# A three-stage block on one core: merge gates biased during the choosing of keys, two of them loaded early, joining's first two tiles reordered

## The chip, the core and the metric

The kernel runs on one core of a Trainium2 chip. The core has TensorE (matrix products, called PE in the profile, with its weight loads apart as PEld), VectorE (DVE), ScalarE (ACT), GpSimd (POOL), and SyncE (SP), which here only issues transfers. All five run their own instruction lists and meet at semaphores. The metric is device time in microseconds for one execution of the whole program, as a median over runs. Before the change it is 3973.13 us over 3 runs (3967.18 to 3975.65).

## The reference

Two transformer blocks in a row, in float32, over 1024 rows of 1024 columns. Only the first block's middle is touched:

```python
proj = jnp.matmul(h, w_in[l])
(fq, fk, fv, flog, dq, dk, dv, iq, ik, iw, g_fox, g_dsa) = jnp.split(proj, split_at, axis=-1)
...
merged = (jax.nn.sigmoid(g_fox + b_gate[l, :D]) * jnp.matmul(out_fox, w_proj_fox[l])
          + jax.nn.sigmoid(g_dsa + b_gate[l, D:]) * jnp.matmul(out_dsa, w_proj_dsa[l]))
x = x + gt1 * jnp.matmul(merged, w_out[l])
h2 = rmsnorm(x, norm2_g[l]) * (1.0 + sc2) + sh2
```

The gates `g_fox` and `g_dsa` are 2048 columns of `proj`. A routed mixture of 32 experts and a second block follow.

## The kernel before

The rows are cut into NT = 8 tiles of 128, the columns into chunks of CH = 512. Each stage is a block with one hand-written program for each engine, and all engines meet at a barrier between two stages. The order of work is the order in which these programs are written; there is no planner except the table of `side_work`.

**choose** (214 to 678 us of the profile) finds the 256 best keys of each row. DVE does it: for each tile, 32 rounds of MAX8 (L667) and MATCH_REPLACE8 (L668), and `gather` (L649, L652) adds up the next tile's scores between them. PE has little to do for this, so `side_work` gives it 64 tasks on the side: 8 small ones, and 7 chunks of `proj` by 8 tiles. The last four chunks (tasks 32 to 63) are the gates. Each task is 8 products of 128x512 (16 in the profile's count), a copy by ACT into one of four buffers `ch_out`, and a store to DRAM issued by ACT (L601). POOL meanwhile weighs the 8 chunks of a vector-matrix product in four steps each (L628 to L634), and PE turns each result into columns (`turn`). The stage is over when ACT has seen all stores land and DVE has read the last turned columns.

**attending** (678 to 996 us) runs two attentions, 32 units each (the sparse one, then the forgetting one, `fox`), through DVE, ACT and PE. SP loads `w_proj` when the sparse half's scores are reduced, one `plain` tile (the forgetting decay) for each tile of the second half, and `w_out` in two pieces of 2 MB, the second after the last unit (L772).

**joining** (997 to 1338 us) works tile by tile. `merge(t, c)` is 8 products (L1190) for column half c, which the profile counts as 16, `mix(t, c)` on DVE (L1390 to L1393) multiplies them by the opened gates and adds the two; `flip_m(t)` transposes the result on PE (L1200), `project(t, c)` multiplies it by `w_out` (L1213), `residual` on DVE adds it to x, ACT squares it and takes the root, `scale_rows` on DVE scales it, `flip_x` transposes it (L1223), and `logit` scores it for the router. The gate of a tile goes through SP (load), POOL (`bias_gate`, L1336) and ACT (`open_gate`, the sigmoid, L1291). In DVE's gaps `weigh` (L1417, L1420) builds the second block's modulation from chunks `w_mod` of 2 MB, loaded by SP one after the other into a single buffer, each when the one before has been weighed (`load_mod`, L1160): one chunk for each tile, and a second one for odd tiles.

**experts** (1338 us on) reads its first weights into `space` and `aT`, which SP loads in joining's last part.

## Time and profile before

| what | value |
|---|---|
| median of 3 runs | 3973.13 us (3967.18 to 3975.65) |
| the profiled execution | 3977.49 us, of which its span is 3975.5 us |
| PE busy | 3741.8 us, 94% of the span |
| DVE, ACT, POOL busy | 1737.1, 952.4, 458.2 us |
| granted clock of PE, mean | 0.947 of full speed |

"Busy" is the sum of an engine's instruction times. Two parts matter here: the end of choose (660 to 680 us) and the start of joining (995 to 1075 us). Each is read on a timeline, engine by engine: start, duration, what it is, and in brackets how long the engine stood idle before it and what released it. The granted clock is 1.00 at full speed (2.4 GHz) and 0.50 at the lower level (1.2 GHz).

### The profile page before, as it was taken

To read this page: it belongs to the slowest core of one execution; us is meant where nothing else is said; L and a number is where in the kernel's file an instruction comes from. 1 tells how busy PE (TensorE), PEld (TensorE's weight loads), DVE (VectorE), ACT (ScalarE), POOL (GpSimd) and SP (SyncE) were. 2 spreads that over 40 slices of the span, in tenths; PEclk is the share of its full clock that TensorE was granted. 3 is DMA by queue.
4 is the path that set the end of the run, shared out by engine and by line. 5 is a ranking of instruction groups with operands and counts; after the bars stand their busy time and mean duration, and the time that the engine had idled before them with its cause. 6 is when DMAs were issued, how large, how long until landed. Compare 5 with 4: busy or idle time off the path is not lost. (4 is left out here: it accounts for less than half of the span.)

```text
span 3975.5 us, 45903 instructions
## 1 busy us (share of the span) xinstructions
PE 3741.8 (94%) x18108; PEld 1997.1 (50%) x18108; DVE 1737.1 (44%) x2905; ACT 952.4 (24%) x1981; POOL 458.2 (12%) x348
## 2 busy tenths in 40 slices
PE   6999999999799699999977999999898999999999
PEld 3554444555455444444435457876655444444444
DVE  2479998655455100000012334555353343343246
ACT  2311111544122122222113312222243311111001
POOL 0032231311210211010111111211000000000000
PEclk8979999999899799999986999999899999999999
DMA  4213232121645489898956222222113111111434
GB/s 172 74 35 119 77 138 81 30 61 36 219 146 194 166 335 335 330 341 328 342 201 236 90 71 88 94 81 86 52 35 116 41 43 43 43 43 43 130 109 158
DMA packets 294008, 533.04 MB, mean 134 GB/s; under 512 B 24132, under 2 KB 103060, under 8 KB 291518
## 3 DMA queue, kind: packets, MB, share of 16 engines
q1 hardware_dynamic: 272574, 472.17, 34.3%
q0 software_dynamic: 11952, 43.52, 2.7%
...
q14 instruction: 54, 0.44, 0.0%
...
## 5 line engine op out<-in xcount | busy, mean ns | idle before, releaser
L561 PE MATMUL ch_side<-aT,space 128*128 128x512 f32 x896 | 391.9, 596 | 0.0
L1738 DVE TENSOR_SCALAR ex_y<-ex_y,ex_entry 128x1024 f32<-128x1024 f32 x32 | 41.1, 1284 | 639.7 <-PE ex_y L1658 639.7
L561 PEld LDWEIGHTS ch_side<-aT,space 128*128 128x128 f32 x896 | 168.9, 191 | 213.2 <-issue 210.5
L1642 PE MATMUL ex_a<-space,ex_xT 128*128 128x512 f32 x512 | 228.5, 600 | 6.2 <-ACT ex_xT L1709 6.2
L2962 PE MATMUL en_bank<-en_h,en_up 128*128 128x512 f32 x528 | 233.8, 593 | 0.0
L1658 PE MATMUL ex_y<-aT,ex_actT 128*128 128x512 f32 x512 | 227.9, 599 | 0.7 <-ACT ex_actT L1721 0.7
L1642 PE MATMUL ex_b<-space,ex_xT 128*128 128x512 f32 x512 | 225.0, 593 | 0.0
L2124 PE MATMUL mx_duo<-mx_chunks,mx_region 128*128 128x512 f32 x384 | 183.6, 635 | 0.0
L667 DVE MAX8 ch_best<-ch_score 128x8 f32<-128x384 f32 (+5 forms) x192 | 171.6, 894 | 6.1
L668 DVE MATCH_REPLACE8 ch_score<-ch_best,ch_score 128x384 f32<-128x384 f32 (+5 forms) x192 | 168.1, 875 | 0.0
L1642 PEld LDWEIGHTS ex_a<-space,ex_xT 128*128 128x128 f32 x512 | 98.5, 193 | 130.3 <-issue 130.3
L2962 PEld LDWEIGHTS en_bank<-en_h,en_up 128*128 128x128 f32 x528 | 100.4, 190 | 125.6 <-issue 125.6
L2962 PE MATMUL en_bank<-en_h,en_mixed_up 128*128 128x512 f32 x352 | 158.3, 593 | 0.0
L2071 PE MATMUL mx_duo<-mx_late 64*64 64x64 f32 (+1 forms) x3632 | 146.7, 226 | 6.8 <-DVE mx_late L2703 5.7
L1658 PEld LDWEIGHTS ex_y<-aT,ex_actT 128*128 128x128 f32 x512 | 96.0, 193 | 109.8 <-issue 108.7
L1642 PEld LDWEIGHTS ex_b<-space,ex_xT 128*128 128x128 f32 x512 | 95.0, 190 | 107.5 <-issue 107.5
L1709 ACT ACTIVATE ex_xT<-ex_x,modT,ex_gain 128x128 f32<-128x128 f32 x264 | 95.6, 467 | 206.3 <-PE ex_x L1647 206.3
L2071 PEld LDWEIGHTS mx_duo<-mx_late 64*64 64x64 f32 (+1 forms) x3632 | 121.9, 136 | 35.4 <-issue 30.7
L3257 DVE TENSOR_TENSOR en_region<-en_region,en_bank 128x512 f32<-128x512 f32 x88 | 58.5, 685 | 157.9 <-PE en_bank L2962 66.6
L2126 PE MATMUL mx_duo<-mx_chunks,mx_region 128*128 128x256 f32 x512 | 123.2, 396 | 4.4 <-DMA mx_chunks<-w_in 4.4
L3257 DVE TENSOR_TENSOR en_part<-en_part,en_bank 128x512 f32<-128x512 f32 x88 | 58.5, 686 | 151.5 <-ACT en_part L3133 75.5
L2128 PE MATMUL mx_duo<-mx_region,mx_chunks 128*128 128x512 f32 x256 | 119.8, 623 | 4.5 <-DMA mx_chunks<-w_in 4.5
...
## 6 DMA issues: line engine op xcount, KB each, us to landing
space<-exp_w SPq DMA_DIRECT2D x64, 2048.0 KB, 12.6
aT<-exp_w SPq DMA_DIRECT2D x32, 2048.0 KB, 13.9
en_up<-w_down SPq DMA_DIRECT2D x132, 256.0 KB, 3.6
space<-w_ada SPq DMA_DIRECT2D x12, 2048.0 KB, 8.3
mx_x<-proj_padded SPq DMA_DIRECT2D x96, 256.0 KB, 3.6
space<-ada_w SPq DMA_DIRECT2D x8, 2048.0 KB, 14.1
aT<-w_in SPq DMA_DIRECT2D x7, 2048.0 KB, 8.6
proj<-ch_out ACTq DMA_DIRECT2D x56, 256.0 KB, 2.0
```

What stands on the lines that cost most here:

```text
L561: last = nc.tensor.matmul(side_ps[i % 2][:, 0:width], hT[:, k, t * P:(t + 1) * P], by[:, k, 0:width], start=k == 0, stop=k == KD - 1)
L667: chain(nc.vector.max(best[:, :], sc))
L668: chain(nc.vector.match_replace(sc, best[:, :], sc, CHOSEN))
L1642: last = nc.tensor.matmul(ps[:, :], xT[b][:, k, :], w13[b][s][:, k, :], start=k == 0, stop=k == KD - 1)
L1658: last = nc.tensor.matmul(y_ps[:, c:c + CH], actT[:, k, :], w2[b][:, k, c:c + CH], start=k == 0, stop=k == F // P - 1)
L1709: last = nc.scalar.activation(xT[b][:, k, :], x_ps[:, k, :], ACT.Identity, bias=shift[:, k:k + 1], scale=gain[:, k:k + 1])
L2071: mm = lambda out, a, b, start=True, stop=True: nc.tensor.matmul(out, a, b, start=start, stop=stop)
L2124: last = nc.tensor.matmul(ps[:, :], hT[:, k, t * P:(t + 1) * P], w_qkv[c][:, k, :], start=k == 0, stop=k == KD - 1)
L2126: last = nc.tensor.matmul(ps[:, 0:256], hT[:, k, t * P:(t + 1) * P], w_half[c][:, k, :], start=k == 0, stop=k == KD - 1)
L2128: last = nc.tensor.matmul(ps[:, :], w_half[c // 2][:, k, (c % 2) * P:(c % 2 + 1) * P], hT[:, k, t * CH:(t + 1) * CH], start=k == 0, stop=k ...
L2962: last = nc.tensor.matmul(to[:, :], a[:, k, :], b[:, k, :], start=k == 0, stop=k == HK - 1)
L3257: TT(C[a][b], C[a][b], up_bank(i, m)[:, :], op).then_inc(joined, 1)
```

## The change

1. In choose, POOL adds the bias to each gate task's output in `ch_out` before it is stored (`add_bias`, 32 times 128x512). SP, not ACT, issues these 32 stores. POOL's weighing steps are now tied to the tasks: step s of vector n follows task 8 + 7n + 1 + s. The bias, 1 MB, is loaded at choose's start and no longer at joining's.
2. In attending, the gates of tile 0 are loaded behind `w_proj`, the gates of tile 1 after the last scores. `w_out` comes in four pieces of 1 MB; the last three are no longer held until the last unit is weighted, only until the last scores.
3. In joining, POOL adds no bias. SP's first load is the first chunk `w_mod`. PE does `merge(1, 0)` before `flip_m(0)`, and DVE weighs its first chunk after `mix(0, 1)`, not before it. The load of the first expert's w1 waits for the second last `project` as well, since the buffers have moved.

```diff
+        gate_bias = sb("gate_bias", [P, 2 * D])
+        bias_loaded, biased = g.sem("ch_bias_loaded"), g.sem("ch_biased")
...
+        gate_at = lambda kind, n: columns[n] - C_GATE if kind == "column" and columns[n] >= C_GATE else None
+        gates = [i for i, (kind, n, t) in enumerate(tasks) if gate_at(kind, n) is not None]
...
+            sp.dma_start(gate_bias[:, :], row_bcast(g.d["b_gate"][0], 2 * D)).then_inc(bias_loaded, 16)
             for i, (kind, n, t) in enumerate(tasks):
+                if i in gates:
+                    c = columns[n]
+                    sp.wait_ge(biased, gates.index(i) + 1)
...
-                act.wait_ge(side_copied, i + 1)
-                act.dma_start(rows(g.d["proj1"])[:, t, c:c + width], out[i % OUTS][:, 0:width]).then_inc(stored[i % OUTS], 16)
+                if i not in gates:
+                    act.wait_ge(side_copied, i + 1)
+                    act.dma_start(rows(g.d["proj1"])[:, t, c:c + width], out[i % OUTS][:, 0:width]).then_inc(stored[i % OUTS], 16)
...
-            for n in range(len(vectors)):
-                pool.wait_ge(g.vector_loaded, 16 * (n + 1))
-                if n >= 2:
-                    pool.wait_ge(turned, n - 1)
-                TT = nc.gpsimd.tensor_tensor
-                TT(w_vector, w_vector, g.cT[:, 0:KD].unsqueeze(2).broadcast_to([P, KD, CH]), ALU.mult).then_inc(weighed, 1)
-                pool.wait_ge(weighed, 4 * n + 1)
-                TT(w_vector[:, 0:4, :], w_vector[:, 0:4, :], w_vector[:, 4:8, :], ALU.add).then_inc(weighed, 1)
-                pool.wait_ge(weighed, 4 * n + 2)
-                TT(w_vector[:, 0:2, :], w_vector[:, 0:2, :], w_vector[:, 2:4, :], ALU.add).then_inc(weighed, 1)
-                pool.wait_ge(weighed, 4 * n + 3)
-                TT(row[n % 2][:, :], w_vector[:, 0, :], w_vector[:, 1, :], ALU.add).then_inc(weighed, 1)
+
+            def weigh(n, step):
+                if step == 0:
+                    pool.wait_ge(g.vector_loaded, 16 * (n + 1))
+                    TT(w_vector, w_vector, g.cT[:, 0:KD].unsqueeze(2).broadcast_to([P, KD, CH]), ALU.mult).then_inc(weighed, 1)
+                    return
+                pool.wait_ge(weighed, 4 * n + step)
+                if step < 3:
+                    half = KD >> step
+                    TT(w_vector[:, 0:half, :], w_vector[:, 0:half, :], w_vector[:, half:2 * half, :], ALU.add).then_inc(weighed, 1)
+                else:
+                    if n >= 2:
+                        pool.wait_ge(turned, n - 1)
+                    TT(row[n % 2][:, :], w_vector[:, 0, :], w_vector[:, 1, :], ALU.add).then_inc(weighed, 1)
+
+            def add_bias(i):
+                _, n, _ = tasks[i]
+                c = columns[n] - C_GATE
+                if i == gates[0]:
+                    pool.wait_ge(bias_loaded, 16)
+                pool.wait_ge(side_copied, i + 1)
+                TT(out[i % OUTS][:, :], out[i % OUTS][:, :], gate_bias[:, c:c + CH], ALU.add).then_inc(biased, 1)
+
+            for i in range(NT, len(tasks)):
+                if i in gates:
+                    add_bias(i)
+                n, step = divmod(i - NT, 7)
+                if 1 <= step <= 4 and n < len(vectors):
+                    weigh(n, step - 1)
 
         @block.vector
...
+            gate = joining_gates(space)
+            gate_v = rows(g.d["proj1"])[:, :, C_GATE:C_GATE + 2 * D]
...
+            sp.dma_start(gate[0], gate_v[:, 0, :]).then_inc(g.first_gates[0], 16)
...
-            sp.dma_start(w_out[0], out_v[:, :, 0:CH]).then_inc(g.out_loaded[0], 16)
-            sp.wait_ge(weighted, U)
-            sp.dma_start(w_out[1], out_v[:, :, CH:D]).then_inc(g.out_loaded[1], 16)
+            sp.dma_start(w_out[0][0], out_v[:, 0:4, 0:CH]).then_inc(g.out_loaded[0], 16)
+            for a in range(2):
+                sp.wait_ge(scored[a], U)
+            sp.dma_start(gate[1], gate_v[:, 1, :]).then_inc(g.first_gates[1], 16)
+            sp.dma_start(w_out[0][1], out_v[:, 4:8, 0:CH]).then_inc(g.out_loaded[0], 16)
+            for half in range(2):
+                sp.dma_start(w_out[1][half], out_v[:, 4 * half:4 * half + 4, CH:D]).then_inc(g.out_loaded[1], 16)
...
-    w_out = [space[:, a * D:(a + 4) * D].rearrange("p (k n) -> p k n", n=CH) for a in (12, 0)]
+    w_out = [[space[:, a * D:(a + 2) * D].rearrange("p (k n) -> p k n", n=CH) for a in halves] for halves in ((12, 4), (0, 2))]
     return w_proj, w_out
+
+
+def joining_gates(space):
+
+    return [space[:, a * D:(a + 2) * D] for a in (14, 6)]
...
-            load_gate(0)
-            load_gate(1)
...
+            load_mod(0)
...
+            sp.wait_ge(projected, 2 * NT - 1)
...
-                pe.wait_ge(out_loaded[c], 16)
+                pe.wait_ge(out_loaded[c], 32)
...
-            for t in range(NT):
-                merge(t, 0)
+            merge(0, 0)
+            merge(0, 1)
+            merge(1, 0)
+            flip_m(0)
+            for t in range(1, NT):
                 if t >= 2:
+                    merge(t, 0)
                     flip_x(t - 2)
                 merge(t, 1)
                 if t >= 2:
                     logit(t - 2)
-                if t >= 1:
-                    project(t - 1, 0)
+                project(t - 1, 0)
                 flip_m(t)
-                if t >= 1:
-                    project(t - 1, 1)
+                project(t - 1, 1)
...
-                act.wait_ge(biased, t + 1)
+                act.wait_ge(g.first_gates[t % 2], 16)
+                if t >= 2:
+                    act.wait_ge(gate_loaded[t % 2], 16 * (t // 2))
...
-            def bias_gate(t):
-                pool.wait_ge(gate_loaded[t % 2], 16 * (t // 2 + 1))
-                nc.gpsimd.tensor_tensor(gate[t % 2][:, :, :], gate[t % 2][:, :, :], gate_bias[:, :, :], ALU.add).then_inc(biased, 1)
-
-            chain = g.chain(pool)
-            pool.wait_ge(bias_loaded, 16)
-            bias_gate(0)
...
-                if t + 1 < NT:
-                    bias_gate(t + 1)
...
-                weigh("first", t)
+                if t >= 1:
+                    weigh("first", t)
                 mix(t, 1)
+                if t == 0:
+                    weigh("first", t)
...
+            dve.wait_ge(iota, 6)
```

PE at joining's start, before. `jn_bank` are PSUM banks: 0 and 1 take `merge(t, 0)`, 2 and 3 `merge(t, 1)`; the transposes are `flip_m(0)`.

```order
L1190 MATMUL jn_bank1<-dsa,aT 128x512 x4
L1190 MATMUL jn_bank2<-dsa,aT 128x512 [waits proj_loaded1]
L1190 MATMUL jn_bank2<-dsa,aT 128x512 x3
L1190 MATMUL jn_bank3<-dsa,aT 128x512 x4
L1200 MATMUL jn_bank6<-ident,jn_merged0 128x128 [waits jn_mixed]
L1200 MATMUL jn_bank6<-ident,jn_merged0 128x128 x3
L1200 MATMUL jn_bank7<-ident,jn_merged0 128x128 x4
L1190 MATMUL jn_bank0<-dsa,aT 128x512 [waits jn_taken,proj_loaded0]
L1190 MATMUL jn_bank0<-dsa,aT 128x512 x3
```

The same place now.

```order
L1227 MATMUL jn_bank1<-dsa,aT 128x512 x4
L1227 MATMUL jn_bank2<-dsa,aT 128x512 [waits proj_loaded1]
L1227 MATMUL jn_bank2<-dsa,aT 128x512 x3
L1227 MATMUL jn_bank3<-dsa,aT 128x512 x4
L1227 MATMUL jn_bank0<-dsa,aT 128x512 [waits jn_taken,proj_loaded0]
L1227 MATMUL jn_bank0<-dsa,aT 128x512 x3
L1227 MATMUL jn_bank1<-dsa,aT 128x512 x4
L1237 MATMUL jn_bank6<-ident,jn_merged0 128x128 [waits jn_mixed]
L1237 MATMUL jn_bank6<-ident,jn_merged0 128x128 x3
```

The first half of tile 1's merge stands ahead of the transposes of tile 0, and waits for `jn_taken` there.

DVE at the same place, before. The rows with `jn_bank` and `jn_merged` are `mix`, those with `jn_acc` are `weigh`.

```order
L1390 TENSOR_TENSOR space<-space,jn_bank0 128x512 [waits jn_opened,jn_product,chain8528]
L1391 TENSOR_TENSOR space<-space,jn_bank1 128x512
L1393 TENSOR_TENSOR jn_merged0<-space 128x512 [waits jn_taken]
L1417 TENSOR_SCALAR jn_acc0<-space,cT 128x512 [waits jn_mod_loaded]
L1420 SCALAR_TENSOR_TENSOR jn_acc0<-space,cT,jn_acc0 128x512 [waits jn_weighed] x7
L1390 TENSOR_TENSOR space<-space,jn_bank2 128x512 [waits jn_opened,jn_product]
L1391 TENSOR_TENSOR space<-space,jn_bank3 128x512
L1393 TENSOR_TENSOR jn_merged0<-space 128x512 [waits jn_taken]
L1390 TENSOR_TENSOR space<-space,jn_bank0 128x512 [waits jn_opened,jn_product]
```

DVE now.

```order
L1422 TENSOR_TENSOR space<-space,jn_bank0 128x512 [waits jn_opened,jn_product,chain8585]
L1423 TENSOR_TENSOR space<-space,jn_bank1 128x512
L1425 TENSOR_TENSOR jn_merged0<-space 128x512 [waits jn_taken]
L1422 TENSOR_TENSOR space<-space,jn_bank2 128x512 [waits jn_opened,jn_product]
L1423 TENSOR_TENSOR space<-space,jn_bank3 128x512
L1425 TENSOR_TENSOR jn_merged0<-space 128x512 [waits jn_taken]
L1449 TENSOR_SCALAR jn_acc0<-space,cT 128x512 [waits jn_mod_loaded]
L1452 SCALAR_TENSOR_TENSOR jn_acc0<-space,cT,jn_acc0 128x512 [waits jn_weighed] x7
L1422 TENSOR_TENSOR space<-space,jn_bank0 128x512 [waits jn_opened,jn_product]
```

The two `weigh` rows have moved behind the second half of `mix` for tile 0; nothing else of DVE's order changes in this stage but one wait near its end.

POOL in choose, between the weighing of the third and the fourth vector, before. `ch_row` are the weighed rows.

```order
L628 TENSOR_TENSOR space<-space,cT 128x4096 [waits ch_turned,vector_loaded]
L630 TENSOR_TENSOR space<-space 128x2048 [waits ch_weighed]
L632 TENSOR_TENSOR space<-space 128x1024 [waits ch_weighed]
L634 TENSOR_TENSOR ch_row1<-space 128x512 [waits ch_weighed]
L628 TENSOR_TENSOR space<-space,cT 128x4096 [waits ch_turned,vector_loaded]
```

POOL now, from the fourth vector's first step on.

```order
L638 TENSOR_TENSOR space<-space,cT 128x4096 [waits vector_loaded]
L643 TENSOR_TENSOR space<-space 128x2048 [waits ch_weighed]
L655 TENSOR_TENSOR ch_out0<-ch_out0,ch_gate_bias 128x512 [waits ch_side_copied,ch_bias_loaded]
L643 TENSOR_TENSOR space<-space 128x1024 [waits ch_weighed]
L655 TENSOR_TENSOR ch_out1<-ch_out1,ch_gate_bias 128x512 [waits ch_side_copied]
L647 TENSOR_TENSOR ch_row1<-space 128x512 [waits ch_turned,ch_weighed]
L655 TENSOR_TENSOR ch_out2<-ch_out2,ch_gate_bias 128x512 [waits ch_side_copied]
L655 TENSOR_TENSOR ch_out3<-ch_out3,ch_gate_bias 128x512 [waits ch_side_copied]
L655 TENSOR_TENSOR ch_out0<-ch_out0,ch_gate_bias 128x512 [waits ch_side_copied]
L655 TENSOR_TENSOR ch_out1<-ch_out1,ch_gate_bias 128x512 [waits ch_side_copied]
L638 TENSOR_TENSOR space<-space,cT 128x4096 [waits vector_loaded]
```

Between the steps stand the additions of the bias, each behind the copy of its task, so that a step now waits for the tasks ahead of it.

SP across the end of attending and the start of joining, before.

```order
L752 DMA space<-decay_line 128x8x128 [waits ad_restored] x6
L770 DMA space<-w_out 128x8x512 [waits ad_restored]
L772 DMA space<-w_out 128x8x512 [waits ad_weighted]
L76 UNCONDITIONAL_BRANCH
L1141 UNCONDITIONAL_BRANCH [waits barrier_Pool_Activation_PE_DVE_SP_release]
L1149 DMA jn_gate_bias<-b_gate 128x2048
L1144 DMA space<-proj1 128x2048 x2
L1147 DMA jn_x0<-x 128x1024
```

SP now.

```order
L801 DMA space<-w_out 128x4x512 [waits ad_restored]
L804 DMA space<-proj1 128x2048 [waits ad_scored1,ad_scored0]
L805 DMA space<-w_out 128x4x512
L807 DMA space<-w_out 128x4x512 x2
L76 UNCONDITIONAL_BRANCH
L1181 UNCONDITIONAL_BRANCH [waits barrier_Pool_Activation_PE_DVE_SP_release]
L1192 DMA space<-w_ada_2 128x8x512
L1187 DMA jn_x0<-x 128x1024
L1187 DMA jn_x1<-x 128x1024
```

Gates and `w_out` are asked for before the barrier, and the first chunk `w_ada_2` stands first behind it, ahead of x and the router's small tensors.

## Rows read from the trace of the kernel before

**Rows 1.** Windows: stretch, length, then busy us (x instructions) of each engine, PE clock.

```profile
1020.00:1035.00 15.00, 1.54 (x7) 1.54 (x8) 8.56 (x12) 1.91 (x1) 0.37 (x1) 0.50 0.44 153
...
1100.00:1125.00 25.00, 25.00 (x79) 12.85 (x78) 14.28 (x20) 8.81 (x14) 5.63 (x3) 0.93 0.37 124
```

**Rows 2.** Timeline of PE, joining's start: start us, us, what, [idle before <-releaser].

```profile
999.26 13.90 PE L1190 MATMUL jn_bank<-dsa,aT 128*128 128x512 f32 x32
...
1033.46 1.97 PE L1200 MATMUL jn_bank<-ident,jn_merged 128*128 128x128 f32 x8 [20.31 <-DVE jn_merged L1393]
...
1064.77 7.03 PE L1190 MATMUL jn_bank<-dsa,aT 128*128 128x512 f32 x16
...
1072.01 1.09 PE L1223 MATMUL jn_bank<-ident,jn_xn 128*128 128x128 f32 x8 [0.21 <-DVE jn_xn L1408]
```

**Rows 3.** Timeline of ACT, the same stretch.

```profile
997.36 1.28 ACT L1291 ACT_TABLE_LOAD   x1 [2.65 <-PEq L1073]
...
1015.03 1.91 ACT L1291 ACTIVATE space<-space 128x2048 f32<-128x2048 f32 x1 [16.39 <-POOL space L1336]
```

**Rows 4.** Timeline of POOL, the same stretch.

```profile
1010.50 4.50 POOL L1336 TENSOR_TENSOR space<-space,jn_gate_bias 128x2048 f32<-128x2048 f32 x1 [51.40 <-DMA space<-proj]
```

**Rows 5.** Timeline of DVE, the same stretch.

```profile
1017.08 0.69 DVE L1390 TENSOR_TENSOR space<-space,jn_bank 128x512 f32<-128x512 f32 x1 [16.21 <-ACT space L1291]
...
1025.49 0.49 DVE L1417 TENSOR_SCALAR jn_acc<-space,cT 128x512 f32<-128x512 f32 x1 [4.57 <-DMA space<-w_ada]
...
1026.01 5.48 DVE L1420 SCALAR_TENSOR_TENSOR jn_acc<-space,cT,jn_acc 128x512 f32<-128x512 f32 x7
...
1066.77 0.69 DVE L1401 TENSOR_TENSOR jn_bank<-jn_bank,jn_gate 128x512 f32<-128x512 f32 x1
...
1071.01 0.16 DVE L1406 RECIPROCAL jn_stat<-jn_stat 128x1 f32<-128x1 f32 x1 [2.82 <-ACT jn_stat L1307]
```

**Rows 6.** Transfers issued from 960 to 1110 us: count, KB each, median us to landing.

```profile
space<-w_ada SPq DMA_DIRECT2D x5, 2048.0 KB, 8.0
```

**Rows 7.** Page, transfers of the whole run, in the same columns.

```profile
aT<-w_in SPq DMA_DIRECT2D x7, 2048.0 KB, 8.6
...
proj<-ch_out ACTq DMA_DIRECT2D x56, 256.0 KB, 2.0
```

**Rows 8.** Timeline of PE, end of attending and first expert.

```profile
980.38 1.99 PE L818 MATMUL ad_s<-space 64*128 64x512 f32 x8
...
1344.81 8.81 PE L1642 MATMUL ex_a<-space,ex_xT 128*128 128x512 f32 x16 [3.14 <-ACT ex_xT L1709]
```

**Rows 9.** Timeline of SP's queue in attending.

```profile
846.52 88.04 SPq L752 DMA_DIRECT2D space<-decay_line  x6
```

**Rows 10.** Timeline of PE at choose's end.

```profile
674.91 0.95 PE L112 MATMUL ch_mod<-ch_one,ch_row 128*128 128x1 f32 x8
...
678.34 0.49 PE L818 MATMUL ad_s<-at_dkT,dsa 64*128 64x128 f32 x4 [2.48 <-PEq L76]
```

**Rows 11.** Timeline of ACT at choose's end.

```profile
675.12 0.58 ACT L599 COPY ch_out<-ch_side 128x512 f32<-128x512 f32 x1 [6.28 <-PE ch_side L561]
```

**Rows 12.** Timeline of DVE at choose's end.

```profile
675.97 0.19 DVE L674 TENSOR_TENSOR modT<-ch_mod,biasT 128x32 f32<-128x32 f32 x1 [0.26 <-PE ch_mod L112]
```

**Rows 13.** Lines of POOL in choose: group, count | busy us, mean ns | idle before.

```profile
L634 POOL TENSOR_TENSOR ch_row<-space 128x512 f32<-128x512 f32 x8 | 12.5, 1563 | 0.6
```

**Rows 14.** Lines of DVE from 595 to 613 us, POOL busy.

```profile
L667 DVE MAX8 ch_best<-ch_score 128x8 f32<-128x1024 f32 x7 | 8.6, 1228 | 0.2
```

**Rows 15.** Lines of DVE from 620 to 660 us, POOL idle.

```profile
L667 DVE MAX8 ch_best<-ch_score 128x8 f32<-128x1024 f32 x16 | 19.6, 1228 | 0.6
```

**Rows 16.** Timeline of DVE in choose, two pairs of gather.

```profile
458.30 6.58 DVE L652 SCALAR_TENSOR_TENSOR ch_score<-ch_relu,at_wi,ch_score 128x896 f32<-128x896 f32 x2
...
481.20 2.41 DVE L652 SCALAR_TENSOR_TENSOR ch_score<-ch_relu,at_wi,ch_score 128x896 f32<-128x896 f32 x2
```

**Rows 17.** Timeline of POOL in choose.

```profile
451.61 7.02 POOL L628 TENSOR_TENSOR space<-space,cT 128x4096 f32<-128x4096 f32 x1 [45.73 <-DMA space<-ada_w]
```

23 lines of the change are left out of this document (12 added, 11 removed).

## The prediction

> **What bounds the kernel now.** I read three things in turn: the windows, the timelines of joining's start, and the timelines of choose's end. In the windows of joining [rows 1] PE is busy for all of 1100 to 1125 us (25.00 of 25.00), while DVE has 14.28 us and POOL 5.63: from there on PE's own work sets the pace, and what another engine saves is worth nothing. The stretch from 1020 to 1035 us is the exception: PE has 1.54 us of work in 15, at a granted clock of 0.50.
>
> PE's timeline [rows 2] shows the gap. Both halves of tile 0's merge run from 999.26 to 1013.1, and the next instruction is `flip_m(0)` at 1033.46, after 20.31 us of idle time laid to DVE. Read it back: POOL's bias starts only at 1010.50, when the gates have landed, and takes 4.50 [rows 4]; ACT's sigmoid runs from 1015.03 for 1.91 [rows 3]; DVE's `mix` starts at 1017.08 [rows 5]. Then DVE waits 4.57 us for its first chunk `w_mod`, which stands in front of the second half of `mix`, and weighs it from 1025.49 to 1031.5. So two waits on transfers and 6.0 us of DVE work lie between merge and flip.
>
> In choose, PE and DVE end together: PE's last products end at 675.86 [rows 10], and DVE's last instruction, at 675.97, had waited 0.26 us for them [rows 12]. What ends the stage is the last store: the copy of task 63 ends at 675.70 [rows 11], a store of that size takes 2.0 us from issue to landing [rows 7], and PE's first work of the next stage stands at 678.34 after 2.48 us of idle time [rows 10].
>
> **Joining, step by step.** I lay the new order on the old durations. A merge or a project is 7.03 us with its tail [rows 2]; back to back it is half of 13.90, so 6.9. Eight transposes take 0.9 before the next can start (of 1.09). A `mix` is three instructions of about 0.69, overlapped, 2.0; `weigh` is 0.49 + 5.48, 6.0; `residual` is two of 0.69, 1.4 [rows 5]. A chunk of 2 MB lands 8.0 us after its issue [rows 6].
>
> - Gates: the last scores end at 982.4 [rows 8]. Then four transfers of 1 MB are issued, gates first; two chunks of 2 MB would need about twice 8.0 at the most, so all is there by 998.4, and the gates of tile 1 by about 990. ACT opens tile 0 after its table load, 997.36 + 1.28 + 1.91 = 1000.6. PE's first half merge ends at 1006.2, so the gate is no longer late.
> - PE: merge(0,0), (0,1), (1,0) run through from 999.3 to 1020.0. DVE mixes the second half from 1013.2 to 1015.2 and weighs chunk 0 until 1021.2. That chunk is now SP's first load, issued at about 997.4, landed at 1005.4.
> - flip_m(0) to 1020.9, merge(1,1) to 1027.8, project(0,0) to 1034.7.
> - What is late next is chunk 1: it can be asked for only at 1021.2, when chunk 0 is weighed. It lands at 1029.2 and is weighed at 1035.2; mix(1,1) ends at 1037.2. PE waits 2.5 us, flips, does project(0,1), and starts merge(2,0) at about 1045.1. It was 1064.77 before: a lead of 19.6.
> - Chunk 2 is asked for at 1035.2, lands at 1043.2, is weighed at 1049.2; residual(0,1) ends at 1050.6; ACT's square and root take 2.8 (DVE waited 2.82 for them, [rows 5]); the scaling about 0.9 more. flip_x(0) can start at 1054.4, after 2.3 us of waiting, where it waited 0.21 before [rows 2]. It stood at 1072.01: **the lead is 17.6 us**.
>
> From there both kernels do the same work in the same order, and PE is full. The only edits left are POOL's biases, 4.5 us for each tile, off the path. So the lead stays to the end. I take 17.0, since the loads of chunk 1 and of the gates of tile 2 are now issued together.
>
> On that pair: in choose each load of `w_in` has another 2 MB issued directly behind it, and still lands in 8.6 us against 8.0 [rows 6, 7]. So I charge 0.6 us for it. The Trainium skill (DMA: Bandwidth & Descriptors, section Queues, rings and completion order) says that descriptors of one ring are taken in order, which agrees with the row; the same page says in Issuing engines are not separate DMA queues that transfers interleave, and if this pair did, 3 MB would have to land for the first, 12 us instead of 8, and the sum would be 4 us smaller. The page speaks of different issuers there, and here both come from SP.
>
> The w1 load of the first expert now waits for project(7,0). PE's first expert product waited on ACT, not on a load [rows 8], and the routing lies between the two. In attending, the 1 MB of early gates is issued ahead of the next `plain` tile, which is asked for only at 846.52 [rows 9], 15 us behind the `w_proj` loads. I cost both at nothing. If the cover failed, `plain` would be late by at most one 1 MB load, 4 us (half of 8.0).
>
> **Choose, step by step.** Added: 32 additions of 128x512 on POOL. The nearest row is the last step of the weighing, the same shape, 1563 ns [rows 13], so 50 us of POOL work beside 460 us of the stage; POOL has room. The place that counts is the last task: copy ends at 675.70 as before, then 1.3 to 1.6 us of POOL, then SP's issue instead of ACT's. The stage ends about **1.4 us later**, bounds 1.2 to 2.
>
> The other cost is on DVE. Its `gather` reads two tiles of SBUF. The pair at 458.30 took 6.58 us, the pair at 481.20 the same work in 2.41 [rows 16]; POOL's multiplication of 7.02 us lay across the first [rows 17]. So a gather can lose 4.2 us to POOL. The picks can't: MAX8 takes 1228 ns on average both with POOL busy and with POOL idle [rows 14, 15]. After task 32 there are 8 pairs of gather, and the weighing steps now fall elsewhere: the stall at 458 goes, others come, and each bias may cost up to 1.6. Net I take zero; the bounds are a loss of 8 us (two more stalls of 4.2) and no gain, for PE has no idle time left to give and ends at 675.86 anyhow. The first 3 us of a loss are hidden by the later store.
>
> The Trainium skill (SBUF — State Buffer, section SBUF: two separate sides) has this as an exclusive lock between GpSimd and a DVE instruction with two SBUF inputs or in a 2-port mode: who starts first holds it for the whole instruction. By that rule each of the 16 gathers after task 32 could meet one addition, 16 times 1.6 = 26 us, if all collided; the two pairs shown agree with it, one held and one not.
>
> **Sum.** Minus 17.0, plus 1.4, plus 0: minus 15.6. Against the profiled execution of 3977.49 us that is 3961.9. The median shown is 4.4 us lower, 3973.13, so the forecast for the median is 3957.5, 0.4% faster.
>
> **Rivals.**
> - *Collisions in choose.* Three or four gathers more than before are held by POOL, 4 us each, less the 3 that the store hides: 9 to 10 us. Time 3967. For it: 50 us more of POOL work and a stall of 4 us already there. Against: the long steps are not longer or more. 9%.
> - *Transfers at joining's start stay the bound.* Chunk 0 and chunk 1 land late, because w_out and the gates (4 MB) go out just before them and x and the router's tensors behind. If each lands 4 us late, the waits at flip_m(1) and flip_x(0) grow by that: the lead is 17 - 8 = 9, time 3965. For it: three loads in a chain with DVE's weighing. Against: 8.0 is the median of loads that had neighbours too. 11%.
> - *Slower.* POOL's additions hold the picks. DVE is the co-bound of choose, so if each of 32 additions stops MAX8 or MATCH_REPLACE8 for its own 1.56 us, the picks end 50 us later, 47 after the hidden 3, and the kernel takes 3973 - 17 + 47 = 4003. It decides from 20 us of stalls on, thirteen additions. Against: the equal means of MAX8; for it, only that no addition with a tile and a bias beside MATCH_REPLACE8 stands in a row above. 3%.
> - *It does nothing measurable:* PE's clock eats the lead. After the gap PE ran at 0.50, and later windows stand at 0.93 [rows 1]; if the low stretches fall otherwise, several us go either way. 7%.
>
> **How the numbers follow.** 70% for the forecast, with its own range 3952 to 3963. A difference under 0.2%, 8 us, can't be told from none by this measurement, so the line for faster is 3965.2. The forecast lies below it; of the two first rivals about half does, which makes 0.70 + 0.10, and of the clock case some. Faster 0.85, same 0.11, slower 0.04. The range for 8 in 10 reaches from 3951 (the whole 17.6, no loss, and the run's scatter) to 3966.
>
> **What would show it.** Right: flip_m(0) within 2 us of merge(1,0), a wait of PE of 2 to 4 us before flip_m(1) laid to DVE, one of about 2 before flip_x(0), and flip_x(0) 56 us after the first merge instead of 72.8; no low clock in 1013 to 1035; MAX8 still at 1228 ns; PE's first product of attending 2.5 + 1.4 us after the last of choose. Wrong: gather groups of 896 and 1024 columns with clearly higher means, PE waiting for a load in joining, or `ad_e` waiting for `ad_decay`.

## The result, and the profile after

The changed kernel takes 3953.87 us (median of 7 runs) where the kernel before takes 3966.90 in the same comparison: 0.9956 of its time, interval 0.9942 to 0.9970, so 0.44% faster. One of the seven runs took 4910.72 us at a granted clock of 0.734, and the ratio, here and below, is formed without such slow runs (`orders_only` has one of 6414.6 us) and not from the two medians, whose quotient is 0.9967. The forecast was 3957.5 with a range from 3951 to 3966. The profiled execution took 3950.93 us, its span is 3948.8. The median of the first three runs, the number that stands against the 3973.13 of the kernel before, is 3950.93 as well, 0.07 below the lower end of the range.

PE's timeline at joining's start, in the columns of [rows 2]:

```profile
1000.30 20.77 PE L1227 MATMUL jn_bank<-dsa,aT 128*128 128x512 f32 x48
1020.91 1.04 PE L1237 MATMUL jn_bank<-ident,jn_merged 128*128 128x128 f32 x8
...
1038.11 1.76 PE L1237 MATMUL jn_bank<-ident,jn_merged 128*128 128x128 f32 x8 [2.43 <-DVE jn_merged L1425]
1039.66 8.09 PE L1250 MATMUL jn_bank<-space,jn_mT 128*128 128x512 f32 x16
...
1056.66 1.10 PE L1260 MATMUL jn_bank<-ident,jn_xn 128*128 128x128 f32 x8 [2.04 <-DVE jn_xn L1440]
```

The 20.31 us of idle time ahead of `flip_m(0)` are gone: three merges run through (20.77) and the flip follows without a wait. Two small waits stand later, 2.43 and 2.04 us. `flip_x(0)` (L1260) starts 56.36 us after the first merge. In [rows 2] it started 72.75 us after. This distance, from here on **M**, is the measure that I use for the joining's start in every kernel below, since nothing later disturbs it. It repeats well where the joining is the same: 56.36, 55.98 and 56.27 in three profiles of the changed one, 49.82 twice in another, but 72.75 and 71.70 in the two of the kernel before. One profile stands behind each other M, so differences under about 1 us say little.

ACT's and DVE's timelines (against [rows 3] and [rows 5]) and SP's queue:

```profile
999.70 3.71 ACT L1332 ACTIVATE space<-space 128x2048 f32<-128x2048 f32 x2
```

```profile
1014.24 0.69 DVE L1422 TENSOR_TENSOR space<-space,jn_bank 128x512 f32<-128x512 f32 x1 [4.79 <-PE jn_bank L1227]
...
1016.68 5.48 DVE L1452 SCALAR_TENSOR_TENSOR jn_acc<-space,cT,jn_acc 128x512 f32<-128x512 f32 x7
...
1030.13 0.49 DVE L1449 TENSOR_SCALAR jn_acc<-space,cT 128x512 f32<-128x512 f32 x1 [6.05 <-DMA space<-w_ada]
...
1045.50 0.49 DVE L1449 TENSOR_SCALAR jn_acc<-space,cT 128x512 f32<-128x512 f32 x1 [6.12 <-DMA space<-w_ada]
```

```profile
998.39 0.37 SPq L1192 DMA_DIRECT2D space<-w_ada  x1
...
1001.98 4.12 SPq L1198 DMA_DIRECT2D jn_w<-router_w_exp  x1
...
1022.19 0.38 SPq L1192 DMA_DIRECT2D space<-w_ada  x1
1022.61 0.58 SPq L1184 DMA_DIRECT2D space<-proj  x1
1036.16 0.38 SPq L1192 DMA_DIRECT2D space<-w_ada  x1
```

Both sigmoids run at 999.70, before the first product is there. DVE now waits for PE at 1014.24, where before it waited for ACT. Chunk 0 of `w_mod` is SP's first load, chunk 1 is asked for at 1022.19 and weighed from 1030.13: this is the chain that makes the wait of 2.43. Chunk 2 follows the same way, asked for at 1036.16 and weighed from 1045.50.

At choose's end, PE and POOL (against [rows 10] and [rows 11]):

```profile
674.34 0.95 PE L112 MATMUL ch_mod<-ch_one,ch_row 128*128 128x1 f32 x8
679.06 0.80 PE L853 MATMUL ad_s<-at_dkT,dsa 64*128 64x128 f32 x4 [3.77 <-PEq L76]
```

```profile
675.20 1.26 POOL L655 TENSOR_TENSOR ch_out<-ch_out,ch_gate_bias 128x512 f32<-128x512 f32 x1 [5.59 <-ACT ch_out L608]
```

The bias of the last task lies between copy and store, and PE's idle time at the barrier grew from 2.48 to 3.77 us, by 1.3. The groups of POOL and DVE in choose (group, count | busy us, mean ns | idle before):

```profile
L655 POOL TENSOR_TENSOR ch_out<-ch_out,ch_gate_bias 128x512 f32<-128x512 f32 x32 | 41.7, 1302 | 169.8 <-ACT ch_out L608 169.8
```

```profile
L695 DVE MAX8 ch_best<-ch_score 128x8 f32<-128x1024 f32 x32 | 39.3, 1228 | 1.1
```

MAX8 is at the 1228 ns of [rows 14, 15]. Now the whole run, by stages. Each figure is the distance between the starts of PE's first products of two stages, in the profiled execution of each kernel (choose ends where PE's last product for task 63 starts; the barrier column is from there to the first product of attending):

| us | choose | barrier | attend | join | experts | mixer, first part | second part | ending |
|---|---|---|---|---|---|---|---|---|
| before | 460.1 | 3.8 | 319.1 | 347.4 | 766.3 | 305.3 | 619.2 | 931.2 |
| after | 461.8 | 5.2 | 319.3 | 328.3 | 762.3 | 301.4 | 618.6 | 931.1 |

The spans differ by more than joining explains: 19.1 us there, and 7.9 in the experts and the mixer, where both kernels have the same code. That is the first thing to be settled.

### The profile page after: what moved, and what is told of

It reads as the page before. It is cut to its first block and busy times, and to the rows that moved or that the text cites. A ratio compares the mean times of both kernels' runs of the same rounds, so it can differ in the third digit from the quotient of the medians.

```text
span 3948.8 us, 45937 instructions
## 1 busy us (share of the span) xinstructions
PE 3729.0 (94%) x18108; PEld 1988.6 (50%) x18108; DVE 1716.2 (43%) x2905; ACT 952.3 (24%) x1981; POOL 459.4 (12%) x372
```

## Experiments

Theory A: the gain is the end of the 20 us gap at joining's start, it takes the transfers to bring it, and the 7.9 us further down are scatter between executions of one kernel. Theory B: the change also does something to the later stages. Within A, the parts are to be priced: the bias in choose, the early gates, the place of the chunk, the orders of PE and DVE. All kernels were timed in five rounds against the kernel before.

### The same two kernels again

No edit.

> The kernel before, unchanged, run and profiled again, to see how much two executions of one kernel differ and where. Between the two profiles so far the first product of the experts stood 18.1 us earlier after the change, but the first of the mixer 22.1 and that of the ending 26.6, in code that is the same in both. If that extra 8.5 us is scatter of executions (theory A), two profiles of this same kernel differ by several us in experts and mixer too, and its ratio is 1.000 within 0.1%. If the extra comes from the change (theory B), the two profiles of the kernel before agree to 1 us from the first expert to the end.

Measured: 0.9995 (0.9981 to 1.0008), median 3966.34 us. The stages: joining 344.6, experts 762.7, mixer's first part 301.4. So the 766.3 and 305.3 of the first profile are not the kernel's: its repetition has the values of the changed kernel. The granted clock goes with it: in the 70 us ahead of the mixer's first product it was 0.60 in the first profile and 0.69 in the repetition, and 0.67 in the changed kernel.

> The changed kernel again. Theory A (what the change brings is 17 to 18 us in joining less about 2 in choose; the rest was scatter): ratio 0.9962, 15 us less; joining 18 us shorter again from its first product to the first expert, experts and mixer within the scatter of the kernel before. Theory B (the later stages gain too): ratio 0.994 and 22 us or more.

Measured: 0.9952 (0.9933 to 0.9971), 3949.20 us. Experts 762.7, mixer 302.5. Joining took 321.1, 7 us less than in the first profile of the same kernel, with M 55.98 instead of 56.36 and the waits 2.21 and 1.87: the start is reproduced within 0.4 us. The 7 us lie behind it, and PE's granted clock accounts for them: 0.05 of 160 us is about 8 us, by this estimate. The windows show 160 us in which PE is busy throughout, in the columns of [rows 1], first of `after`, then of `after_again`:

```profile
1060.00:1220.00 160.00, 160.00 (x520) 84.20 (x519) 74.88 (x123) 44.51 (x70) 4.25 (x8) 0.95 0.47 165
```

```profile
1060.00:1220.00 160.00, 160.00 (x544) 84.48 (x543) 77.63 (x128) 46.85 (x73) 5.31 (x10) 1.00 0.48 169
```

Behind `flip_x(0)` joining takes 265.1 us in `after_again` and 271.3 to 276.5 in the thirteen other profiles of this study, those of the kernel before among them (274.7 and 272.9). So `after_again` is the exception, and joining as a whole is to be compared with care. Theory B falls. The levels 766 and 305 come back in the profiles of `double_bias` (766.3, 305.4) and of `bias_only` (766.0, 305.0), whose code there is again the same. In both the clock was 0.60 in the same 70 us.

### DVE's old order in the changed kernel

The changed kernel weighs tile 0's first chunk behind both halves of `mix(0)`. This one weighs it between them, as before.

```diff
-                if t >= 1:
-                    weigh("first", t)
+                weigh("first", t)
                 mix(t, 1)
-                if t == 0:
-                    weigh("first", t)
```

> The changed kernel with DVE's old order: the first chunk is weighed between the two halves of mix for tile 0. My account of joining says that the chain that is late now is chunk 1, which can be asked for only when chunk 0 is weighed. DVE stands idle for 4.8 us where the weighing would go. So chunk 1 should be asked for 6 us earlier less 1.1 for the landing of chunk 0, the waits of 2.4 us before the transposes of tile 1 and of 2.0 before flip_x(0) should go, and with them the low clock behind the first (1.8 us): 4 to 6 us faster than the changed kernel, ratio 0.995 to before. Rival: the order on DVE doesn't matter, since loads come late anyway: same as the changed kernel.

Measured: 0.9934 (0.9916 to 0.9952), 3941.09 us: the lowest ratio of the study, though those of `late_gates` and `chunk_last` below can't be told from it. PE's timeline, same columns:

```profile
997.23 20.77 PE L1227 MATMUL jn_bank<-dsa,aT 128*128 128x512 f32 x48
...
1032.44 1.04 PE L1237 MATMUL jn_bank<-ident,jn_merged 128*128 128x128 f32 x8
...
1047.05 1.04 PE L1260 MATMUL jn_bank<-ident,jn_xn 128*128 128x128 f32 x8
```

And DVE's:

```profile
1006.81 5.47 DVE L1452 SCALAR_TENSOR_TENSOR jn_acc<-space,cT,jn_acc 128x512 f32<-128x512 f32 x7
...
1018.03 0.69 DVE L1422 TENSOR_TENSOR space<-space,jn_bank 128x512 f32<-128x512 f32 x1 [3.83 <-PE jn_bank L1227]
...
1020.60 0.49 DVE L1449 TENSOR_SCALAR jn_acc<-space,cT 128x512 f32<-128x512 f32 x1 [0.56 <-DMA space<-w_ada]
```

PE has no idle time left up to `flip_x(0)`, M is 49.82, 6.5 us less. The weighing falls into time in which DVE waits for PE's merge(0,1) anyway (4.79 us in the changed kernel), chunk 1 is asked for 15.1 us after the first merge and not 21.9, and DVE's wait for it falls from 6.05 to 0.56. So of the change's parts the new order of DVE costs 6.5 us of M; with the chunk's early load it was no longer needed. The times agree, 3941.09 against 3949.20 us for `after_again` in the same comparison, though the two intervals still touch.

### Old orders, with the loads of the change

`weigh_between`, and PE's order as before too:

```diff
-            merge(0, 0)
-            merge(0, 1)
-            merge(1, 0)
-            flip_m(0)
-            for t in range(1, NT):
+            for t in range(NT):
+                merge(t, 0)
...
-                project(t - 1, 0)
+                if t >= 1:
+                    project(t - 1, 0)
                 flip_m(t)
```

> The changed kernel with both old orders, of PE and DVE: only the bias, the loads and their places are new. Account: the chunk lands at about 1007, mix(0,0) ends at 1009.4, weighing ends at 1015.4, mix(0,1) at 1017.4, so PE waits about 3 us at flip_m(0) (1014.2 to 1017.4) and not 20; then chunk 1 is early and no other wait follows. Joining is then 1 to 2 us shorter than in the changed kernel, ratio 0.996. Rival: the order of PE is a main part of the gain: then this loses 7 us or more of it, ratio 0.998.

Measured: 0.9949 (0.9930 to 0.9968), 3947.53 us. PE:

```profile
1014.45 1.09 PE L1237 MATMUL jn_bank<-ident,jn_merged 128*128 128x128 f32 x8 [3.13 <-DVE jn_merged L1423]
1015.38 15.60 PE L1227 MATMUL jn_bank<-dsa,aT 128*128 128x512 f32 x32
```

`flip_m(0)` waits 3.13 us, the two merges behind it take 15.60 where 13.90 is the usual [rows 2], and M is 54.87. Against `weigh_between` PE's new order is worth 5.1 us, 3.1 of wait and 1.7 of products behind it, at a granted clock of 0.90 over the 16.55 us, and 0.2 of rest. Against the kernel before, loads and bias alone bring M from 72.75 to 54.87.

### The new orders alone

The kernel before, with both orders of the change.

```diff
-            for t in range(NT):
-                merge(t, 0)
+            merge(0, 0)
+            merge(0, 1)
+            merge(1, 0)
+            flip_m(0)
+            for t in range(1, NT):
...
-                weigh("first", t)
+                if t >= 1:
+                    weigh("first", t)
                 mix(t, 1)
+                if t == 0:
+                    weigh("first", t)
```

> The kernel before with nothing new but the two orders (PE merges the first half of tile 1 before it transposes tile 0, DVE weighs its first chunk after both halves of mix). By the timeline of before: the gates are late as ever, so merge(1,0) waits about 5 us for them; the transposes follow without a wait; then the first chunk ends late (weighed at 1031.5), chunk 1 with it, and PE waits 7 to 8 us at the transposes of tile 1 and about 2 at flip_x(0). Joining is 7 us shorter, ratio 0.998. Rival (the orders bring the gain, as the change's own words put them last and as a part): 15 us or more, ratio 0.996.

Measured: 0.9996 (0.9985 to 1.0007), 3962.85 us: less gain than I expected. M is 69.74 instead of 72.75 and 71.70. PE:

```profile
1015.51 9.99 PE L1190 MATMUL jn_bank<-dsa,aT 128*128 128x512 f32 x16 [4.85 <-DVE space L1393]
...
1048.07 1.97 PE L1200 MATMUL jn_bank<-ident,jn_merged 128*128 128x128 f32 x8 [7.96 <-DVE jn_merged L1395]
```

DVE and POOL:

```profile
1036.50 9.59 DVE L1422 SCALAR_TENSOR_TENSOR jn_acc<-space,cT,jn_acc 128x512 f32<-128x512 f32 x7
```

```profile
1038.48 4.70 POOL L1338 TENSOR_TENSOR space<-space,jn_gate_bias 128x2048 f32<-128x2048 f32 x1 [21.09 <-DMA space<-proj]
```

The gap is only cut into pieces, 4.85 and 7.96, since the gate is as late as before. What I had not seen: the bias of a later tile, which the orders leave on POOL, falls beside the weighing. The same seven instructions take 9.59 us instead of 5.48, 4.1 more, with 4.70 us of POOL across them. That is the kind of hold that [rows 16] shows in choose.

### The bias alone

The changed kernel's choose, with everything else as before: old orders, gates of the first tiles asked for at joining's start, the chunk last, `w_out` in four pieces, of which three are held until the values are weighted. That is 3 MB held where the kernel before holds 2, and the bias's 1 MB no longer stands behind them, so that as much as before (6 MB with gates and x) is asked for ahead of the router's tensors. This run is therefore not the bias alone in every respect.

```diff
-            for a in range(2):
-                sp.wait_ge(scored[a], U)
-            sp.dma_start(gate[1], gate_v[:, 1, :]).then_inc(g.first_gates[1], 16)
+            sp.wait_ge(weighted, U)
...
-            load_mod(0)
+            for b in range(2):
+                sp.dma_start(gate[b][:, :, :].rearrange("p a b -> p (a b)"), rows(g.d["proj1"])[:, b, C_GATE:C_GATE + 2 * D]).then_inc(g.first_gates[b], 16)
             load_x(0)
...
+            load_mod(0)
```

> Only the moved bias: the changed kernel with both old orders, the gates of tiles 0 and 1 loaded at joining's start, the first chunk asked for last, and w_out's last three pieces held until the last unit as before. Account: POOL's 4.5 us go from the gate's way, so the first mix starts 3 to 6 us earlier, but the second waits for the chunk as before; flip_m(0) 2 to 4 us earlier, less 1.3 at choose's end: ratio 0.9985 to 1.000. Rival (the bias on POOL was what held joining's start): most of the gain is here, ratio 0.996.

Measured: 1.0002 (0.9993 to 1.0011), 3964.98 us.

```profile
1034.25 1.97 PE L1236 MATMUL jn_bank<-ident,jn_merged 128*128 128x128 f32 x8 [16.83 <-DVE jn_merged L1422]
```

```profile
1014.06 0.69 DVE L1419 TENSOR_TENSOR space<-space,jn_bank 128x512 f32<-128x512 f32 x1 [9.30 <-ACT space L1329]
...
1026.27 0.49 DVE L1446 TENSOR_SCALAR jn_acc<-space,cT 128x512 f32<-128x512 f32 x1 [10.20 <-DMA space<-w_ada]
```

```profile
1002.74 10.65 SPq L1196 DMA_DIRECT2D jn_w<-router_w_exp  x1
...
1018.36 0.43 SPq L1189 DMA_DIRECT2D space<-w_ada  x1
```

`mix(0,0)` starts earlier, 10.95 us after the first merge instead of 17.8 ([rows 2, 5]), and nothing comes of it: DVE only waits longer for the chunk, 10.20 us instead of 4.57. SP's queue is held for 10.65 us at one of the router's tensors, so the chunk is issued at 1018.36, 15.3 us after the first merge (in the kernel before the same tensor held SP for 11.84 us, and the chunk was issued at 1016.69, 17.4 after). Once the bias is off the path, the chunk is the bound. M is 69.13, 3.6 less than the 72.75 before and 2.6 less than the 71.70 of its repetition, and the barrier's 1.3 us are paid for it.

### When the gates are loaded, and where the chunk stands

`late_gates` is `weigh_between` with the gates of tiles 0 and 1 asked for at joining's start, ahead of the chunk:

```diff
-            sp.dma_start(gate[0], gate_v[:, 0, :]).then_inc(g.first_gates[0], 16)
...
-            sp.dma_start(gate[1], gate_v[:, 1, :]).then_inc(g.first_gates[1], 16)
...
+            for b in range(2):
+                sp.dma_start(gate[b][:, :, :].rearrange("p a b -> p (a b)"), rows(g.d["proj1"])[:, b, C_GATE:C_GATE + 2 * D]).then_inc(g.first_gates[b], 16)
             load_mod(0)
```

> weigh_between, but the gates of tiles 0 and 1 are loaded at joining's start, ahead of the first chunk, and not during the attentions. The gates would land by 1006, before the first product is done at 1007.3; the chunk comes 4 us later, which the product that is added on PE still covers. Account: within 1.5 us of weigh_between, joining 321 to 323 us from its first product to the first expert, ratio 0.9935 to 0.994. Rival: the early load is a main part of the gain, then 5 us or more are lost, ratio 0.995 or more.

Measured: 0.9942 (0.9926 to 0.9957), 3941.93 us, M 51.25, one wait of PE, 1.27 us at `flip_x(0)`. The early gates by themselves are worth 1.4 us of M, no more, which is little above what M scatters by.

`chunk_last` is `weigh_between` with the first chunk asked for behind x and the router's tensors:

```diff
-            load_mod(0)
             load_x(0)
...
+            load_mod(0)
             for t in range(NT):
```

> weigh_between, but the first chunk w_mod is asked for last, behind x and the router's small tensors, as in the kernel before. It would be issued at about 1011.5 and land at 1019.5, the weighing would end at 1025.5, PE would wait 6 to 7 us at the transposes of tile 0 and 2 at flip_x(0): 8 to 9 us of the gain are lost, joining 330 us, ratio 0.9955. If the place of this load were unimportant, it would be as weigh_between, 0.9934.

Measured: 0.9939 (0.9925 to 0.9953), 3941.04 us, M 52.87, waits 0.82 and 1.85. My expectation of the loss was too high by more than twice. SP's queue shows why:

```profile
1000.36 0.58 SPq L1197 DMA_DIRECT2D jn_w<-router_w_exp  x1
...
1004.71 14.68 SPq L1192 DMA_DIRECT2D space<-w_ada  x2
```

The transfer that held SP for 10.65 us in `bias_only` takes 0.58 here, so SP reaches the chunk at 1004.71. Each edit alone gives back little, 1.4 and 3.1 us of M, though without any of them M is 14.3 higher (`bias_only` against `old_orders`). So the last two kernels undo them together. `both_late` is `late_gates` with the chunk asked for last, as in `chunk_last`. `all_late` also holds `w_out`:

```diff
-            for a in range(2):
-                sp.wait_ge(scored[a], U)
+            sp.wait_ge(weighted, U)
             sp.dma_start(w_out[0][1], out_v[:, 4:8, 0:CH]).then_inc(g.out_loaded[0], 16)
```

> weigh_between with both edits undone: the gates of tiles 0 and 1 are asked for at joining's start, and the first chunk of w_mod last, behind x and the router's tensors. w_out keeps its early place (asked for when the scores end). Theory Q (what holds SP at the router's tensor is the amount asked for just before it, and the 3 MB of w_out are most of it): SP is held some 3 us instead of the 10.65 of bias_only, the chunk is issued about 10 us after the first merge and lands at 18, is weighed at 24, mix(0,1) ends at 26: PE waits 5 us at flip_m(0), M (flip_x(0) after the first merge) 55 to 57, ratio 0.9945 to 0.9955. Theory G (the gates alone, 2 MB, hold it as long): the chunk is issued 15 us after the first merge and lands at 23, PE waits 10 us at flip_m(0), M about 62, ratio 0.9965.

> both_late, and w_out held until the values are weighted, as before the change. By both theories the queue is now as in bias_only: SP held about 10.6 us, the chunk issued 15 us after the first merge, landed at 23, weighed at 29; PE waits 10 us at flip_m(0), M about 62, ratio about 0.9965. Against bias_only (M 69.13, 1.0002) the rest is PE's new order, worth 7. Theory Q sees 5 to 7 us of M between this and both_late, theory G none.

Measured: `both_late` 0.9967 (0.9952 to 0.9981), 3953.93 us, M 57.81; `all_late` 0.9976 (0.9966 to 0.9987), 3957.06 us, M 63.87. SP's queue and PE in `both_late`:

```profile
1001.85 3.39 SPq L1197 DMA_DIRECT2D jn_w<-router_w_exp  x1
...
1010.22 14.54 SPq L1190 DMA_DIRECT2D space<-w_ada  x2
```

```profile
1026.32 1.97 PE L1237 MATMUL jn_bank<-ident,jn_merged 128*128 128x128 f32 x8 [5.72 <-DVE jn_merged L1425]
```

and in `all_late`:

```profile
999.47 10.65 SPq L1196 DMA_DIRECT2D jn_w<-router_w_exp  x1
...
1015.11 14.41 SPq L1189 DMA_DIRECT2D space<-w_ada  x2
```

```profile
1031.09 1.97 PE L1236 MATMUL jn_bank<-ident,jn_merged 128*128 128x128 f32 x8 [11.62 <-DVE jn_merged L1424]
```

Theory Q holds, theory G falls: the early `w_out` is worth 6.1 us of M when the chunk stands last. Its 3 MB (three loads of 1 MB) then no longer stand in front of the router's tensors, and the chunk is issued 10.4 us after the first merge instead of 16.4. DVE's first `mix` also starts 7.1 us after the first merge and not 12.1, since the gates land sooner, but that changes nothing, for DVE waits for the chunk behind it in both (9.37 and 10.32 us). Both times came out slower than Q had them: 0.9967 where 0.9945 to 0.9955 was expected, 0.9976 where 0.9965 was, and M is 1 to 2 us above the forecasts. With that, M can be walked down from the kernel with the bias alone: 69.13, PE's order 63.87, `w_out` early 57.81, gates early 52.87, chunk first 49.82. DVE's new order then takes it up to 56.36, the changed kernel. The walk goes by M, most of it from one profile a kernel; of the ratios only the first step, 1.0002 to 0.9976, stands clear of its neighbour's interval. Its order matters: with the chunk first, the early gates are worth 1.4 and not 4.9.

### A second addition in choose

The changed kernel, each gate task with one more addition, of zeros, on POOL.

```diff
+                pool.wait_ge(added, gates.index(i) + 1)
+                TT(out[i % OUTS][:, :], out[i % OUTS][:, :], zero[:, :], ALU.add).then_inc(biased, 1)
```

> The changed kernel with a second addition (of zeros) on POOL for each of the 32 gate tasks, 41 us more of POOL work beside the choice of keys. Account: MAX8 and MATCH_REPLACE8 keep their 1228 and 1209 ns, and what is added is the 1.3 us at the stage's end, plus at most a stall or two of gather that stays hidden: ratio 0.9955. Rival (POOL's additions hold the picks): MAX8's mean rises and choose is 20 us or more longer.

Measured: 0.9959 (0.9944 to 0.9973), 3949.72 us. 32 more additions of 1357 ns, 43.4 us of POOL work, and choose takes 462.0 instead of 461.8. Only the barrier moved, from 5.2 to 6.5 us, as the last task's additional step says. MAX8 and MATCH_REPLACE8 at 1024 columns stay at 1228 and 1208 ns. POOL's load in itself doesn't hold the picks. It does hold DVE a little elsewhere: the conversions of the scores take 5.9 us in all instead of 3.1, the gather 2.3 us more, and DVE's last conversion ends at 680.90, 3.9 us behind PE's last product for task 63, where in the changed kernel both end at 674.5. The last store, issued at 680.39, still lands later, so nothing of it shows.

The joining of this profile is the changed kernel's once more, M 56.27, and it shows something that the other two don't:

```profile
1042.64 1.09 PE L1242 MATMUL jn_bank<-ident,jn_merged 128*128 128x128 f32 x8 [2.38 <-DVE jn_merged L1430]
1043.58 7.03 PE L1255 MATMUL jn_bank<-space,jn_mT 128*128 128x512 f32 x16
```

Here the project behind the wait of 2.38 us took the usual 7.03, not the 8.09 or 8.66 of `after` and `after_again`, the wait at `flip_x(0)` was 3.69 us instead of 2.04 or 1.87, and M came out the same.

### Gates first in choose

`weigh_between` with the gates' columns ahead of Q, K and V in the list of tasks, so that they are stored long before the barrier.

```diff
-    columns = [C_FQ, C_FK, C_FV] + list(range(C_GATE, N1, CH))
+    columns = list(range(C_GATE, N1, CH)) + [C_FQ, C_FK, C_FV]
```

> weigh_between, with the four gate chunks put first in choose's list of tasks (8 to 39) and the three others last, so that the stage's last store is one without a bias and is issued by ACT again. Account: the time from the last task's products to the next stage's first goes back from 5.1 to 3.8 us, 1.3 us less; POOL's additions now fall beside the shorter keys, where more gathers are, at most a few us of stalls on DVE, hidden unless DVE ends after PE. So 1 us faster than weigh_between, ratio 0.993. Rival: more gathers are held and choose is 3 us or more longer.

Measured: 1.0002 (0.9988 to 1.0016), 3964.94 us. The whole gain is gone. M is still 49.82: it isn't joining. PE at the barrier:

```profile
673.03 0.95 PE L112 MATMUL ch_mod<-ch_one,ch_row 128*128 128x1 f32 x8
698.34 0.80 PE L853 MATMUL ad_s<-at_dkT,dsa 64*128 64x128 f32 x4 [24.36 <-PEq L76]
```

DVE's conversion of the last scores ends at 697.57, where PE is done at 673.98. The gather's groups in choose, first of the changed kernel (orders in joining don't touch them), then of this one:

```profile
L680 DVE SCALAR_TENSOR_TENSOR ch_score<-ch_relu,at_wi,ch_score 128x768 f32<-128x768 f32 x7 | 7.1, 1019 | 0.5
L680 DVE SCALAR_TENSOR_TENSOR ch_score<-ch_relu,at_wi,ch_score 128x512 f32<-128x512 f32 x7 | 5.3, 751 | 1.1 <-DVE ch_score L696 0.7
```

```profile
L680 DVE SCALAR_TENSOR_TENSOR ch_score<-ch_relu,at_wi,ch_score 128x768 f32<-128x768 f32 x7 | 20.3, 2897 | 0.5
...
L680 DVE SCALAR_TENSOR_TENSOR ch_score<-ch_relu,at_wi,ch_score 128x512 f32<-128x512 f32 x7 | 12.6, 1806 | 3.4 <-issue 2.9
```

One pair in the timelines of DVE and POOL:

```profile
265.65 8.18 DVE L680 SCALAR_TENSOR_TENSOR ch_score<-ch_relu,at_wi,ch_score 128x512 f32<-128x512 f32 x2 [2.91 <-issue]
...
283.73 1.60 DVE L680 SCALAR_TENSOR_TENSOR ch_score<-ch_relu,at_wi,ch_score 128x512 f32<-128x512 f32 x2
```

```profile
265.78 7.49 POOL L638 TENSOR_TENSOR space<-space,cT 128x4096 f32<-128x4096 f32 x1
```

POOL's multiplication of 7.49 us lies across the pair of 8.18; alone such a pair takes 1.60. The six groups of the gather sum to 73.4 us, against 59.9 in the changed kernel, and the conversions of the scores to 10.6 against 3.1, the one of 128x640 alone 4.79. DVE's whole work in choose takes 486.3 us, against 460.9 in `weigh_between`: 16.7 of the 25.4 us are longer instructions (gather and conversions), the other 8.7 are idle time, above all waits for ACT's `ch_relu` at the first tiles, which in `weigh_between` pass while POOL holds the first tile's gather. In the new program POOL's weighing steps stand between the additions, and each addition waits for its task, so moving the gates moved the steps as well, into gathers. This is the mechanism of my first rival, at 20 us instead of the 9 to 10 that I gave it; that it is POOL's hold throughout is read from the timelines, and no run separates the long steps from the additions. It needs a kernel that places POOL's long steps badly; the changed kernel doesn't.

## Why the prediction came out as it did

**The gap and what bounds joining: right.** The gate was taken off the path, chunk 0 too, and PE ran through, as the forecast put it. `flip_m(0)` started without a wait at 20.6 us after the first merge (forecast 20.7).

**What is late next: right.** I named chunk 1 as next, with waits of 2.5 at `flip_m(1)` and 2.3 at `flip_x(0)`. Measured 2.43 and 2.04 (2.21 and 1.87 in the repetition). The lead was forecast as 17.6, taken as 17.0. M fell from 72.75 to 56.36, which is 16.4, or by the means of both pairs of profiles (72.2 and 56.2) 16.0. The missing microsecond is the load of chunk 2. It was asked for 35.9 us after the first merge, as forecast, but DVE could weigh it only 9.34 us after its issue (9.19 and 9.30 in `after_again` and `double_bias`), where the forecast had 8.0. `flip_x(0)` waits for DVE's chain, so the 1.3 us go straight into M. PE's clock was lower behind the first wait: `flip_m(1)` took 1.76 and the project behind it 8.09, instead of 1.04 and 7.03, and `merge(2, 0)` started 47.3 us after the first merge instead of the 45.8 forecast. But that was made good in the wait at `flip_x(0)`: `double_bias` has 1.09 and 7.03 there and the same M. Behind `flip_x(0)` the lead stays, as forecast: the rest of joining takes 271.3 to 276.5 us with the old kernels and the new ones, `after_again` with its higher clock aside.

**The pair of loads: small, as charged, but on the other chunk.** I charged 0.6 us. Chunk 1 was issued at 1022.19, the gates behind it at 1022.61, and DVE began to weigh at 1030.13, 7.94 us after the issue. The Trainium skill's rule that descriptors of one ring are taken in order (DMA: Bandwidth & Descriptors, section Queues, rings and completion order) agrees with this row. The 12 us that interleaving would have made of it did not occur. Chunk 2, with the next gates asked for 1.9 us behind it, took the 9.34 us; what it lost them to is not shown.

**Choose's end: right.** Forecast plus 1.4. The barrier went from 3.8 and 3.9 (two profiles) to 5.2 and 5.1.

**DVE in choose: right for this order of tasks.** Forecast zero, bounds a loss of 8. Choose took 460.1 and 461.5 before, 461.8 and 461.5 after. Doubled additions held DVE's end back by 3.9 us and cost the kernel nothing but the barrier's 1.3. One reading under this forecast was wrong. I laid the multiplication of [rows 17] across the pair of gathers at 458.30, but it ends at 458.63. What lay across the second gather of the pair (459.68 to 464.89) is POOL's next step:

```profile
458.70 5.23 POOL L630 TENSOR_TENSOR space<-space 128x2048 f32<-128x2048 f32 x1
```

The stall of 4.2 us and its price stand, but it was the second step, not the first, that held the gather, and POOL has eight of each.

`gates_first` shows that the bound of 8 was too tight for the mechanism in general, though not for this change.

**The level and the range: this step failed.** The sum was minus 15.6, and the time fell by 0.44% of 3966.9, 17.5 us (by the interval 12 to 23). So the change was sized well, and the step that failed is the level from which it was taken off, and with it the range. It is the sum's last line: "The median shown is 4.4 us lower, 3973.13, so the forecast for the median is 3957.5". I took both the profiled execution and a median of three as the kernel's level. In the later comparisons the kernel before had medians of 3970.42, 3964.73, 3964.73 and 3967.05 us with 17 to 21 runs each, single runs from 3955.6 to 3980.4, so that 3973.13 lies 6.4 us above the mean of these medians. Part of it can be seen: the profile of before carries 3.6 us in the experts and 3.9 in the mixer that its repetition lacks, at a granted clock of 0.60 instead of 0.69 between the two. From 3966.9 the same sum gives 3951.3, against the 3950.93 of the first three runs and the 3953.87 of all seven. And the range's lower end, "the whole 17.6, no loss, and the run's scatter", allowed 0.6 us for the gain and some 6 for the scatter, while the same kernel has joining at 328.3 and at 321.1 in two profiles, at clocks of 0.95 and 1.00. The rival that PE's clock moves several us either way, which I had down at 7%, is not a rival but a width that every case has.

**The slower rival: shown wrong** by `double_bias`. Of the others, transfers as the bound held for the kernels without the early loads (`bias_only`, `all_late`). In this one the chunks still make the waits that are left (2.43 and 2.04 us), but they came 7.94 and 9.34 us after their issue and not 4 us late each.

**Gain by parts.** The bias alone 1.0002, the orders alone 0.9996, bias and PE's order 0.9976, bias and loads 0.9949, all 0.9952 and 0.9956, all but DVE's order 0.9934. Neither the bias (with the old loads and orders) nor the orders alone can be told from nothing, since three things stood one behind the other ahead of the same flip: the gate's bias, the chunk behind a held queue, and DVE's weighing. `weigh_between` and `after_again` have the same joining (321.6 and 321.1) though M differs by 6.2, since the second ran at a clock of 1.00 from 1060 to 1220 us and the first at 0.95. What stays open is what decides that clock from one execution to the next: PE was busy throughout in both.
